# A fused two-block transformer kernel: input DMAs spread anew over two queues, output projections begun inside the attentions' last steps, modulation pieces, splits and evictions placed anew

## The reference, cut to what matters

```python
# block 1
h = rms_norm(x, g_pre_mix); proj = h @ w_in            # 1024 -> 2560: q, k, v, xr, gr
attn = attention(q, k, v, rel_bias)                     # 8 heads of 64, causal, T5 bias
lru = rg_lru(causal_dwconv(xr)) * gelu(gr)              # gates r, i; linear scan over positions
x = x + rms_norm(concat(attn, lru) @ w_out, g_post_mix)
h = rms_norm(x, g_pre_ffn); up = causal_dwconv(h @ w_up)
x = x + rms_norm((gelu(c_g) * c_u) @ w_down, g_post_ffn)
# block 2, twice: mod = silu(c) @ w_ada[i] + b_ada[i] (6 x 1024: shifts, scales, gates)
x = x + g_a * mixer(rmsnorm(x) * (1 + sc_a) + sh_a)     # i = 0: neighborhood attention, 16 heads; i = 1: MLA
x = x + g_f * ffn(rmsnorm(x) * (1 + sc_f) + sh_f)       # i = 0: SwiGLU; i = 1: mixture of 8 experts, top 2
return rmsnorm(x) * final_norm
```

## Time and profile before

| what | us |
|---|---|
| three runs, median | 1415.43 |
| three runs, lowest and highest | 1411.67, 1417.05 |
| the profiled execution, device time | 1419.5 |
| its span, first to last instruction | 1417.7 |
| PE busy | 1320.5 |
| DVE busy | 1076.2 |
| ACT busy | 836.4 |

### The profile page before, as it was taken

How to read it: one execution, slowest core, us unless ns; L and a number is a source line. 1 busy time by engine, 2 the same in 40 slices (tenths; PEclk the granted TensorE clock), 3 DMA queues, 4 the chain that set the end, 5 groups by cost and what they waited for, 6 DMA issues and landing times.

```text
span 1417.7 us, 20384 instructions
## 1 busy us (share of the span) xinstructions
PE 1320.5 (93%) x7614; PEld 1153.8 (81%) x7614; DVE 1076.2 (76%) x1208; ACT 836.4 (59%) x1104; POOL 80.5 (6%) x102
## 2 busy tenths in 40 slices
PE   5888999999899899999966987999999999999996
PEld 5877799987898679998755666989888888889894
DVE  5785799985655477776645447989888988889888
ACT  4653666544545354443334745777777777777774
POOL 0040000002252000000000300000000000000000
PEclk9997999999999999999988996999999999999999
DMA  8782677679833558897632031999999999999992
GB/s 305 247 306 78 235 268 267 238 288 235 179 101 119 193 193 297 297 332 282 220 119 70 14 119 58 342 312 365 315 345 335 331 345 314 354 321 357 322 354 80
DMA packets 192890, 349.13 MB, mean 246 GB/s; under 512 B 23892, under 2 KB 161439, under 8 KB 186551
## 3 DMA queue, kind: packets, MB, share of 16 engines
q1 hardware_dynamic: 188112, 342.49, 70.5%
q10 hardware_dynamic: 4535, 5.17, 1.2%
q0 software_dynamic: 176, 0.56, 0.1%
HBM read 347.12 MB, written 1.06 MB: 246 GB/s over the span
## 4 chain that ended last, share of the span: by engine, by line
PE 85%; DVE 6%; ACT 5%; issue 2%; DMA 1%; ACTq 1%; POOL 0%; DVEq 0%
PE ps L1110 11%; PE ps L663 8%; PE ps L664 8%; PE ps L665 8%; PE ps L1080 8%; PE ps L1082 7%; PE ps L1081 7%; PE ps L676 6%; PE ps L680 6%; PE ps L678 6%; PE ps L762 1%; ACT whi L1145 1%; PE ps L1051 1%; DVE wlo L1627 1%; PE ps L785 1%
## 5 line engine op out<-in xcount | busy, mean ns | idle before, releaser
L1145 ACT ACTIVATE whi<-raw 128x1024 fp32r<-128x1024 f32 (+2 forms) x210 | 218.1, 1052 | 268.2 <-PE ps L680 132.6
L1627 DVE TENSOR_TENSOR wlo<-raw,whi 128x1024 fp32r<-128x1024 f32 (+2 forms) x210 | 252.6, 1225 | 138.3 <-ACT whi L1145 135.8
L663 PE MATMUL ps<-ahi,whi 128*128 128x256 f32 x960 | 278.0, 290 | 8.3 <-DVE alo L1660 8.0
L664 PE MATMUL ps<-alo,whi 128*128 128x256 f32 x960 | 275.2, 287 | 0.0
L665 PE MATMUL ps<-ahi,wlo 128*128 128x256 f32 x960 | 275.0, 286 | 0.0
L1635 DVE TENSOR_TENSOR wlo<-raw,whi 128x1792 fp32r<-128x1792 f32 (+1 forms) x96 | 199.8, 2089 | 24.8 <-ACT whi L1158 23.0
L1158 ACT ACTIVATE whi<-raw 128x1792 fp32r<-128x1792 f32 (+1 forms) x96 | 168.6, 1757 | 63.6 <-PE ps L1082 34.7
L663 PEld LDWEIGHTS ps<-ahi,whi 128*128 128x128 f32 x960 | 188.1, 196 | 12.5 <-issue 10.4
L664 PEld LDWEIGHTS ps<-alo,whi 128*128 128x128 f32 x960 | 188.0, 196 | 0.7 <-issue 0.7
L665 PEld LDWEIGHTS ps<-ahi,wlo 128*128 128x128 f32 x960 | 188.0, 196 | 0.0
L1080 PE MATMUL ps<-whi,hchi 128*128 128x448 f32 x352 | 131.5, 374 | 3.4 <-DVE hclo L2195 2.8
(11 more groups left out here) (322 smaller groups left out, 2574.8 us busy)
## 6 DMA issues: line engine op xcount, KB each, us to landing
raw<-in_moe_w_gu SPq DMA_DIRECT2D x96, 896.0 KB, 6.6
ada<-in_w_ada SPq DMA_DIRECT2D x48, 1024.0 KB, 5.7
raw<-in_moe_w_down SPq DMA_DIRECT2D x32, 1024.0 KB, 6.8
ada<-in_moe_w_gu SPq DMA_DIRECT2D x32, 896.0 KB, 6.7
raw<-in_w_up SPq DMA_DIRECT2D x22, 1024.0 KB, 5.2
raw<-in_ffn_w_gu SPq DMA_DIRECT2D x22, 1024.0 KB, 9.5
ada<-in_moe_w_down SPq DMA_DIRECT2D x16, 1024.0 KB, 7.2
raw<-in_na_w_qkv SPq DMA_DIRECT2D x12, 1024.0 KB, 6.1
```

What stands on the lines that cost most here:

```text
L663: pe.matmul(o, h[:, k, cols], bhi[:, k], start=(k == 0), stop=False)
L664: pe.matmul(o, h[:, k, cols], blo[:, k], start=False, stop=False)
L1145: act.activation(part_of(whi[ck.half], c, q), part_of(raws[ck.slot], c, q), ACT.Copy).then_inc(hi_done, 1)
L1627: ve.tensor_tensor(part_of(wlo[ck.half], c, q), part_of(raws[ck.slot], c, q), part_of(whi[ck.half], c, q).bitcast(F32), ALU.subtract).then ...
```

## The change

- Start: ACT issues ten vector loads; SP issues relb and the other four behind x, no longer waits for the vectors, and takes wr, wi and gvec after chunk 3.
- First stage: chunks are loaded ahead of pieces; 6 pieces instead of 8 in the input projection, the next two in the output projection, so the down projection takes 7 instead of 5; PE's two column sums leave the attention steps for the first norm after it, which has fewer fills.
- ACT evicts a projection before the lru's tanh and exponentials, and values before splits; it asks for the bias table at c = 3; the bias wait on DVE comes after the piece; lru steps come one step earlier; decay is shorter.
- Both output projections: chunks 0 and 1 are put before and between the last two attention steps, in banks that the steps do not use, and in the first one the order of the rows of w_out is changed; `mix_ready` gives way to finer waits; the split of chunk 2 comes before the last step.

The core of the diff:

```diff
-ADA_MIX = [[8, 9], [0, 1]]
-ADA_UP = [{j: [9 + j] for j in range(1, 10)}, {}]
+ADA_IN = 6
+ADA_MIX = [[6, 7], [0, 1]]
+ADA_UP = [{j: [7 + j] for j in range(1, 10)}, {}]
-SUMS1 = {4: 0, 5: 1}
+OUT_ORDER = [0, 4, 6, 2]
+OUT_BANKS = [(0, 6), (4, 6), (0, 6), (4, 6), (4, 6)]
-FILL = {1: (2, 5, 1), 2: (2, 7), 3: (2, 5, 1), 4: (1, 2), 5: (1, 4)}
+FILL = {1: (1, 3, 1), 2: (2, 7), 3: (2, 5, 1), 4: (1, 2), 5: (1, 4)}
+LATE_ROWS = ["b_ada", "w_conv_ffn01", "w_conv_ffn2", "b_conv_ffn"]
...
SP:
                 for j in range(ADA_DOWN[layer], ADA_CHUNKS):
                     load_ada(layer, j)
-                    load(gu + c)
-                    c += 1
+                    if layer or gu + c < W_QKV - 1:
+                        load(gu + c)
+                        c += 1
...
+            sp.dma_start(relb, a["rel_bias"]).then_inc(sem("relb_in"), 16)
             sp.dma_start(cst, a["consts"]).then_inc(sem("cst_in"), 16)
-            sp.wait_ge(sem("rows_in"), 16 * ROW_DMAS)
+            load_rows(LATE_ROWS)
             for c in range(W_UP):
-                if NRAW <= c < NRAW + ADA_FIRST:
+                if c == NRAW:
+                    sp.wait_ge(sem("wri_zero"), 1)
...
+                    sp.dma_start(gvec, a["g_post_mix"][0:1, :].broadcast_to([P, D])).then_inc(sem("gvec_in"), 16)
+                load(c)
+                if NRAW <= c < NRAW + ADA_IN:
                     load_ada(0, c - NRAW)
-                load(c)
...
PE:
+            def output_chunk(first, c, bhi, blo, s, second=None):
+
+                for q in range(2):
+                    begin(first + c, q)
+                    k = 2 * c + q
+                    for t in range(NT):
+                        if second and q == 0 and t == 1:
+                            pe.wait_ge(*second)
+                        m = rows_block(first + c, q, 2, D, k, k == 0, False, bhi, blo, t, outs(s, t))
+                    done(m)
...
+            pe.wait_ge(sem("a_sfree"), HEADS0[1] + 2 * PAIRS[1])
+            pe.wait_ge(sem("a_out"), HEADS0[1] // 2 + 2)
+            output_chunk(W_OUT, 0, *ordered1, 0, (sem("in_free"), 10))
             step1(PAIRS[1])
+            pe.wait_ge(sem("lru_ready"), 2)
+            output_chunk(W_OUT, 1, *ordered1, 0)
             step1(PAIRS[1] + 1)
-            pe.wait_ge(sem("in_free"), 10)
-            pe.wait_ge(sem("mix_ready"), 1)
-            output_projection(W_OUT, KT, *mixes[1], 0)
+            pe.wait_ge(sem("lru_ready"), LT)
+            output_projection(W_OUT, KT, *ordered1, 0, begun=2, last=HEADS0[2] // 2)
+            sum_columns(0, (0,), 3)
+            transposes(1, between=lambda: sum_columns(0, (1,), 3, KT))
             pe.wait_ge(sem("mod_read0"), 1)
-            transposes(1)
...
+            pe.wait_ge(sem("a_sfree"), HEADS0[2] + 2 * PAIRS[2])
+            pe.wait_ge(sem("a_out"), HEADS0[2] // 2 + 4)
+            output_chunk(W_NAO, 0, *mixes[2], 2, (sem("qkv2_free"), 12))
             step2(PAIRS[2])
+            output_chunk(W_NAO, 1, *mixes[2], 2)
             step2(PAIRS[2] + 1)
-            pe.wait_ge(sem("mix_ready2"), 1)
-            output_projection(W_NAO, KT, *mixes[2], 2)
+            output_projection(W_NAO, KT, *mixes[2], 2, begun=2, last=HEADS0[3] // 2)
...
ACT:
             for name, (tile, row, count, _) in VEC.items():
-                ld(rows[row:row + count, tile, :], VEC_SRC[name](a), "rows_in")
...
+                if name not in LATE_ROWS:
+                    ld(rows[row:row + count, tile, :], VEC_SRC[name](a), "rows_in")
...
+                if c >= 8:
+                    values1(c)
+                split(c + 2, (1,) if at_ is not None and c < 8 else (0, 1))
...
-                if c == 4:
+                if c == 3:
                     act.wait_ge(sem("tbl_out"), 16)
...
             turned_pairs(2, PAIRS[2])
+            split(W_NAO + 2)
             turned_pairs(2, PAIRS[2] + 1)
-            down(W_NAO, 4)
+            down(W_NAO, 4, 1)
...
DVE:
-                own.link(ve.memset(q, 1.0 / 17))
-                for n in (15, 13, 11, 9, 7, 5, 3, 1):
-                    own.link(ve.tensor_tensor(q, q, z2, ALU.mult))
-                    own.link(ve.tensor_scalar(q, q, 1.0 / n, None, ALU.add))
-                own.link(ve.tensor_tensor(q, q, z, ALU.mult))
+                own.link(ve.tensor_scalar(q, z2, 1.0 / 17, None, ALU.mult))
+                for n in (15, 13, 11, 9, 7, 5, 3):
+                    own.link(ve.scalar_tensor_tensor(q, q, 1.0 / n, z2, ALU.add, ALU.mult))
+                own.link(ve.scalar_tensor_tensor(q, q, 1.0, z, ALU.add, ALU.mult))
...
-                if 2 <= i < 2 + LT:
-                    lru_late(i - 2)
+                if 1 <= i < 1 + LT:
+                    lru_late(i - 1)
...
+                if c == 1:
+                    ve.wait_ge(sem("c_ready"), 1)
+                    modulate_part(0, 0)
...
+                if 2 <= c <= ADA_IN:
+                    modulate_part(0, c - 1)
                 if c == 5:
                     ve.wait_ge(sem("bias1_in"), 32)
-                if 1 <= c <= ADA_FIRST:
-                    modulate_part(0, c - 1)
...
             step2(PAIRS[2])
+            split(W_NAO + 2)
             step2(PAIRS[2] + 1)
             ve.wait_ge(sem("a_out"), HEADS0[3] // 2)
-            ve.sem_inc(sem("mix_ready2"), 1)
-            ve.wait_ge(sem("mix_ready2"), 1)
             ve.sem_inc(sem("ada_free1"), 1)
-            down(W_NAO, 4, 1, ADA_MIX[1])
+            down(W_NAO, 4, 1, ADA_MIX[1], begun=1)
```

More of the change, by code:

```diff
@@ L740, in output_projection @@
                                 begin(first + c, q)
+                            if last and (t, c, q) == (0, chunks - 1, 0):
+                                pe.wait_ge(sem("a_out"), last)
                             k = 2 * c + q
-                            m = rows_block(first + c, q, 2, D, k, False, k == k_all - 1, bhi, blo, t, outs(t))
+                            m = rows_block(first + c, q, 2, D, k, False, k == k_all - 1, bhi, blo, t, outs(s, t))
                             if t == NT - 1:
@@ L1202, in norm @@
                     act.wait_ge(mm_done, 2 * last)
-                    square(f"r{s - 1}", 1, ps[:, 6:8, :].rearrange("p b n -> p (b n)"))
+                    b = OUT_BANKS[s - 1][1]
+                    square(f"r{s - 1}", 1, ps[:, b:b + 2, :].rearrange("p b n -> p (b n)"))
                 if s == 0:
                     square(s, 1, x[:, 1])
+                    first(0)
                     act.wait_ge(sem("vecs_ready"), 1)
@@ L1332, in _ @@
                         m.then_inc(sem("ri_read"), 1)
+                act.wait_ge(mm_done, 2 * (W_IN + c + 1))
+                b = 4 + c if c < 4 else 6 + c % 2
+                if c >= 8:
+                    if (c, 1) in AT_STEP[1]:
+                        i = AT_STEP[1][c, 1]
+                        turned_pairs(1, i)
+                        pair_exponentials(1, i)
+                    continue
+                if c < 2:
+                    for f in range(2):
+                        k = 2 * c + f
+                        act.activation(lru[0][:, k], ps[:, b, f * S:(f + 1) * S], ACT.Identity,
+                                       scale=wc[:, 3 * LT + k:3 * LT + k + 1], bias=bc[:, k:k + 1])\
+                            .then_inc(sem("tap3"), 1)
+                    continue
+                dst = lru[1] if c < 4 else (qT1, kT1)[c % 2]
+                k = 2 * (c % 2) if c < 4 else 2 * (c // 2 - 2)
+                o = dst[:, k:k + 2, :]
+                i = ps[:, b, :].rearrange("p (f s) -> p f s", f=2)
+                if c in (4, 6):
+                    o, i = o.rearrange("p f (b n) -> p (f b) n", n=P), reversed_in(ps[:, b, :], P)
+                act.activation(o, i, ACT.Gelu_apprx_tanh if c < 4 else ACT.Copy).then_inc(sem("in_free"), 1)
                 if c == 5:
@@ L1368, in _, with lru_hi @@
                     pair_exponentials(1, i)
+            def lru_hi(k):
+                act.wait_ge(sem("lru_out"), k + 1)
+                act.activation(ahi[:, LT + k], lru[0][:, k], ACT.Copy).then_inc(sem("lru_hi"), 1)
+            lru_hi(0)
+            lru_hi(1)
             turned_pairs(1, PAIRS[1])
+            lru_hi(2)
+            lru_hi(3)
+            split(W_OUT + 2)
             turned_pairs(1, PAIRS[1] + 1)
@@ L1395, in gate_biases, with down @@
                     act.dma_start(gate_row[layer][g], src).then_inc(sem("gbias_in"), 16)
-            def down(first, chunks):
-                for c in range(chunks - 2):
+            def down(first, chunks, begun=0):
+                for c in range(begun, chunks - 2):
                     split(first + c + 2)
-            for k in range(LT):
-                act.wait_ge(sem("lru_out"), k + 1)
-                act.activation(ahi[:, LT + k], lru[0][:, k], ACT.Copy).then_inc(sem("lru_hi"), 1)
             sh_a, sc_a, sh_f, sc_f = (mod[:, n * KT:(n + 1) * KT] for n in range(4))
-            down(W_OUT, 4)
+            down(W_OUT, 4, 1)
```

(15 more changed lines are left out.)

120 lines of the change are left out of this document (49 added, 71 removed).

## The result

Changed kernel: 1389.4 us median of six runs (1384.7 to 1393.6) against 1415.7 of six runs of the kernel before; ratio 0.982, 95% interval 0.980 to 0.984. That is 26.3 us faster, and the forecast was 1390.5. The profiled execution took 1393.5 us with a span of 1391.7, 26.0 under the span of before.

The account below looks back on a forecast made before the run. PE, busy 93%, was taken as the bound, with gains only where it is not full. Terms -5.2 - 6.5 - 14.5 + 1.3 - 0.5 - 0.5 = -25.9, rounded to -25, gave 1390.5 us by the median; range 1381 to 1404.

Parts of the forecast that it names:

- tail: From chunk 9's end to the fill after the first output projection: -14.5 us, ends -9 and -15.5.
- the norm: First norm after the first output projection: the column sums move here; +1.3 us, ends 0 and +3.
- the down projection: First down projection: seven modulation pieces instead of five, 4.8 us of DVE in a 5.5 us chunk; change 0.
- start: Up to the first projection matmul: ACT free sooner, vectors landing at 8.0 to 8.5; -5.2 us.
- middle: From there to chunk 9's end: bias and key waits go, POOL wait of 5 us comes; net -6.5 us.
- second norm: Norm before QKV: later bias2a request moves POOL's mask off it; -0.5 us, ends -1.5 and +2.
- second attention: Naive gain of 7.6 us eaten by waiting for layer 1's pieces; -0.5 us, ends -6 and +2.
- rival C: Start bound by transfers, vectors queueing beside 4 MB of weights; head gains 0, total 1395.7 us; chance 0.10.
- A: Second attention gains in full, pieces landing before DVE wants them; 6 us more, 1384.5 us; chance 0.10.
- B: DVE's chain stays the bound through the first attention; middle gains nothing, tail 10; 1401.5 us; chance 0.17.
- D: The change only moves the waits; less than 7 us gained, 1412 us; chance 0.05.
- E: Slower: PE at half clock from first attention until first norm, +33 against -26, 1422 us; chance 0.03.

Follow-up runs that it names:

- run 6: Changed kernel with the evictions of queries and keys behind tanh and exponentials again at chunk 5: 1393.0 us, ratio 0.984.
- run 1: Kernel before with the new start alone: 1409.6 us against 1413.0, ratio 0.9966.
- run 8: Changed kernel with ada buffers freed after attention step 3, weight chunks 1 to 3 held until the vectors landed, POOL's mask after the second norm: 1375.9 us.
- run 11: Changed kernel with early ada buffers, POOL's mask after the second norm, DVE scaling x before vector copies, PE's bias table matmul before vector transposes: 1376.8 us.
- run 7: Changed kernel with the recurrent unit's first late part moved on DVE from attention step 1 to 2: 1388.0 us, ratio 0.9815.
- run 10: Changed kernel with the recurrent unit's three DVE operations of chunk 6 behind the split and modulation piece again: 1393.2 us, ratio 0.985.
- Run 5: Changed kernel with the first attention's first two output chunks after its steps 4 and 5 again: 1399.1 us, ratio 0.9895.
- run 3: Changed kernel with the ada buffers freed after the scores of the second attention's step 3, not after step 9: 1383.6 us, ratio 0.978.

## Why the prediction was right, point by point

**The time, 1390.5 against 1389.4,** is right, and its largest steps are: the bias table's DMA is off the path, the keys' wait is gone (and back in run 6), the tail lost 15.3 us for the 14.5 forecast, the norm gained 0.9 for 1.3, the down projection still hides its pieces, `bias2a` comes 11 us later. But the sum hides terms that were off, and they cancel: start +1.5, middle -3.2, tail -0.8, second norm -1.0, second attention +1.5, and 2.1 us in stages that nothing was to change. That the total came out within 1.1 us is in part luck. So is the frame: the tail, more than half of the sum, was priced on one profile of before, and run 1 shows that stretch 4.6 us shorter in the same code.

**Start, -5.2, measured -3.7 and -3.8.** The failed step is "I let the last vectors land at 8.0 to 8.5, behind x and the constants". The last vector is issued by 4.5 us instead of 6.1, and all are there at 9.20 instead of 8.87: their landing did not follow their issue, it came 4.7 us behind it instead of 2.8. So x's turns gained 2.1 us for the 3.7 of the forecast, and the split's part came as worked out (1.6 for 1.5). What sets the landing stays open. Holding back chunks 1 to 3 moved it by 0.2 (run 8), so it is not those 3 MB; but chunk 0 was asked for ahead of it in every run with the new start, with the DMA engines full, and so rival C's mechanism, a queue beside the weights, is not excluded for this part. Its price, a gain of 0, did not come. What the new start gave was time on ACT's sequencer, and DVE's copies, which stand ahead of x's scaling, then kept 1.7 us of it (run 11). The Trainium skill, "DMA: Bandwidth & Descriptors", section "Issuing engines are not separate DMA queues", puts the use of a second issuing engine at the sequencer's time alone: the runs agree with that. They do not agree with "usually small relative to the DMA itself": here it was 2.1 us of path at x's turns beside 4.9 to 5.0 for x's DMA, since ACT's sequencer issued DMAs until 10.0 us in front of its own first square.

**Middle, -6.5, measured -9.7.** The failed step is "5 if it takes 5.85; I take the upper, since DVE now has its lru operations exactly there". PE waited 1.40. (How 7.1 us on DVE's chain and 5.5 on PE's become 6.5 with that wait, the prediction does not add up.) I had weighed the late part of the recurrent unit, which run 7 shows to be no neighbour of step 0's four POOL operations; the block that the change puts there runs its two-input operations for 2.5 us in place of a split and a piece of 4.7. Run 10 puts these back and has a wait of 4.56 us, near the 5 of the forecast, and the middle then gains 5.7 (chunk 9 ends at 97.46, PE starts at 17.83) for the 6.5 forecast; its stage is 2.4 to 4.1 us longer. So the move of three operations of DVE, which the prediction did not name, carried a quarter to two fifths of the middle's gain. The same rule of POOL and DVE stood in the prediction from the Trainium skill's "SBUF — State Buffer", section "Who interferes with whom"; runs 7 and 10 agree with it (3.55 us beside 2.49 of two-input work, 6.73 beside 4.71), and the mistake was in which instructions I put side by side.

**Tail, -14.5, measured -15.3.** Right in its sum against the profile of before; against run 1's 35.6 us for the same code it would be -10.7. Run 5 says what the chunks inside the steps are worth: 6.7 to 8.4 us, of which 6.2 are waits of PE and the rest mostly matmuls at the half clock behind them. The prediction counted them as cover for 3.25 + 2.04 and called the rest of the steps' time their own; without the chunks, a wait that no row of before showed (3.54) takes the place of the sums.

**Second norm, -0.5, measured -1.5.** The term was too small: the kernel before and run 1 took 14.5 and 15.3 us, the changed kernel and the nine other profiles with its mask 11.8 to 13.0 (mean 12.3). It is left open what the mask costs there.

**Second attention, -0.5, measured +1.0 from the first QKV matmul, and -0.7 from step 0** (over all profiles of the two forms -0.9; ahead of step 0 the changed kernel's profile took 18.9 us and that of before 17.1). Here the unusual step held: the naive gain is there (2.64, 1.57, 0.73 and 0.99 idle are gone), and the wait for layer 1's pieces takes it back, with DVE idle 2.22 + 5.28 for them and PE 6.86 where 5 was forecast (6.86 to 7.29 in all five profiles of this form). The second piece took 10.7 us to land for the 9.6 forecast. Freeing the buffers after step 3 brings it out (run 3, table). What I did not see is that the change's other edits there bring the gain without that bill: the chunks in this attention are a loss of 5.9 us as the change has them. By the whole times the change without them is 4.8 us faster by the medians and 3 by the ratios, whose intervals overlap.

**The rivals.** A needs the pieces early and then gives what it said and more (run 3: 5.8 by medians, 9.0 in the stage). B did not come, as middle and tail both gained, nor did D. E did not come either: the granted clock was 1.00 from 17.85 to 118.35 us, with dense chunks between the steps.

## What to carry to other kernels

When work is pulled ahead of a step to cover its wait, list who is released by the end of that step: an event that fires behind the pulled work is late by all of it, and its DMA's landing time comes on top. Release a buffer at its last reader and not at the end of the stage. Where the clock moves, time a stage between marks with the same work behind them, and over several profiles: here a constant of 19.1 us taken off turned a gain of 2.0 to 2.5 us into 4.7. And where POOL has a short operation on the path, look at which DVE instructions will lie beside it after the edit, not at how many there are.

## What the runs showed of the hardware

- Among the first DMAs a small one takes as long as a large one: in run 8 `relb` (1 KB, issued at 1.25 us) landed 4.8 us behind its issue, x (1 MB, issued at 0.73) 5.0. In the kernel before, where `relb` was issued at 6.10 and the DMA engines were 0.30 busy from 7 to 9 us, it landed 2.8 behind. The fourteen vectors were there at 8.87 to 9.44 in every kernel, whether the last was issued by 4.5 or by 6.1 us, and in run 8 with 3 of the first 4 MB of weights held back until they had landed.
- Four POOL operations on 128x128, 0.41 us each by the pair of 0.82, took 3.55 us, and 6.73 in run 10, where only DVE's order beside them differs. Two took 5.85, and 1.08 or 2.77 with a late part or a split beside them (run 7).
- DVE suffers as well: low parts of 0.69 us took 1.77 while POOL added the mask (12.89 us), and beside splits of DVE the same mask took 15.94.
- Idle PE can cost twice. Behind waits of 3.54, 3.92 and 6.86 us the next matmuls ran at the half clock (1.55, 1.65 and 1.97 us for eight, and ten fills in 6.62, partly at half), behind one of 3.94 the half clock came with the matmuls after them (0.93 for the eight). Behind the waits of up to 1.6 us shown here they ran at full, but for one of 1.24 that followed the 3.54 (1.22 us for two 512-column matmuls, 0.70 in the changed kernel).
